# Three output projections of two model blocks: seven half-size products instead of one full product, and three VectorE steps moved

## The chip, the cores and the metric

The kernel runs on one core of a Trainium2 chip, in one launch. The metric is the device time of that core in microseconds (us). TensorE (PE) multiplies, VectorE (DVE) and ScalarE (ACT) do the element work, and SyncE (SP) issues the transfers from HBM. All data is float32.

## What is computed

A first block (a recurrent mixer and an attention mixer side by side, an output projection, then 64 experts in 8 groups) is followed by a second one (three attentions, gates, an output projection) and a last norm. There are 256 tokens (`S`) of width 1024 (`D`). The places that the change touches:

```python
# first block
y = sigmoid(gate_a) * (o_a @ w_branch_hgrn) + sigmoid(gate_b) * (o_b @ w_branch_mla)
x = x + y @ w_out                       # units wo0, wo1
h = rmsnorm(x, ffn_norm_w)
x = x + hierarchical_moe(h, ...)        # 2 of 64 experts for each token
x = rmsnorm(x, final_norm_w)
# second block
kv = rmsnorm(mem, g_mem) @ w_mem_kv     # its unit xva is computed ahead of the experts
u = gates[0] * ya + gates[1] * yb + gates[2] * yc
x = x + u @ w_out_2                     # units w20, w21
x = rmsnorm(x, g_final)
```

## The kernel before

**Units.** A weight matrix is cut into units of 512 columns: 8 blocks `k` of 128 rows, 2 MB each (`wo0` is the first half of `w_out`, `wo1` the second, `w20` and `w21` those of `w_out_2`). They pass through a ring of four slots (three in the second block); SP asks for a unit when the projection that used its slot is done.

**One list for all engines.** `plan()` writes the steps in one order; each engine runs through the list and does its part of each step, so the order of the list is the order on every engine. `("head", (unit, n))` lets TensorE do the first n products of a unit early. Projections write the psum tiles P0 and P1; `may_fill` makes TensorE wait until such a tile was read. A semaphore `full` says that a tile is written, `empty` that it was read.

**Two forms of a projection.** In the full form a unit is 16 matmuls of 512 columns (for each half `t` of the tokens, 128 each, 8 blocks k) or 32 of 256. A float32 matmul stands in the trace as two records, so 32 records of 512. The units of the list `FAST` use seven products instead (a Winograd scheme: input and weight are each seen as 2 x 2 parts, and 7 products of sums of parts give the 8 products of parts). Each product is 4 matmuls of 256 columns, or 8 of 128: 28 or 56 matmuls, 56 or 112 records. Around them VectorE does:
- `sums` (unit, 0 and 1): sums of the four weight parts, 128 x 1024 each: two in part 0 and one in part 1. In the first block the last factor, `t4`, overwrites a part of the weight, so it is a step of its own, `late`, which waits until products 2 and 1 have read that part (semaphore `made`);
- `halves`: four sums of the input's parts, 128 x 512;
- `merge` (step `proj` on VectorE): seven additions of 128 x 256 that combine the products into the result. ScalarE copies product 1 out of psum for them. The third addition frees the first of the two psum tiles.

The products run in the order 2, 1, 6, 5, 7, 3, 4; product 4 wants `t4`.

**Around the three moved steps.** During ga0 the list has 40 of its 56 matmuls, then `cnorm` (scale a 704-wide tile, transpose it, fill `cT`), the sums of the next unit ga1, ga0's `late`, then the rest of ga0. Before wb0 it has `halves` of `ob`, `gated`, `mnorm` (memT times its weight, 128 x 2048, and two small diagonals), the sums of wb1, and `late("wb0")`.

**From wo0 to the experts.** wo0 and wo1 are in the full form; VectorE adds the psum to `X` (one step of 128 x 1024 for wo0, two of 512 for wo1). `X` is transposed (xT), the router's logits (`rt`, L1444) follow, then 13 of the 16 matmuls of xva, which reads `wxva`; then the `rank` (L1714), for which VectorE must have made the router's mask (L1033), the gather (L739) and the experts' first product (L760).

**The transfers.** The experts' weights are 96 chunks of 4 MB in four buffers. SP asks for chunks 0 and 1 when wa1 and wb1 are read, chunk 2 when wb1 is full, chunk 3 when wo1 is full. `wxva` (1 MB) is asked for behind chunk 1, `fifth` (the first MB of chunk 4) behind chunk 3. The rest of chunk 4 is asked for when TensorE has read half of chunk 0 (`half_used`), and each later one when its buffer is free.

**The end.** w20 and w21 are in the full form, with heads that finish both products of the first 128 tokens first (`w2_tile`), so that their norm and output run beside the second 128. w21's second tile is done in two parts of 256 columns.

## Time and profile before

| | |
|---|---|
| median of three runs | 1581.46 us (1581.41 to 1582.23) |
| the profiled execution | 1581.34 us, its span 1579.5 us |
| TensorE busy | 1258.5 us (80%) |
| VectorE busy | 535.7 us (34%) |
| ScalarE busy | 207.0 us (13%) |
| transfers over the span | 504.48 MB read, 320 GB/s |

Times in the trace are microseconds from the start of the span. The experts take from about 346 to 1243 us; ahead of them is the first block, behind them the second. "PEclk" is the share of its full clock that TensorE was granted. A row of the chain is a piece of the longest path: start, length, what ran. TensorE's records start about 0.15 us ahead of the piece of the chain that they belong to.

### The profile page before, as it was taken

How to read it: one execution, taken by the hardware profiler on the slowest of the kernel's cores; microseconds unless marked ns; L12 is line 12 of the kernel's file. 1: busy time of each engine (PE TensorE's matmuls, PEld its weight loads, DVE VectorE, ACT ScalarE, POOL GpSimd, SP SyncE). 2: the span in 40 equal slices, each digit the busy share in tenths (PEclk: the TensorE clock that was granted, in tenths of full speed). 3: DMA queues.
4: the chain of work that ended last, by engine and by line, in shares of the span. 5: the costliest groups of instructions: out<-in, count | busy, mean ns of one | idle time of the engine just before them, and what ended most of it. 6: DMA issues, size and time to landing. Idle time of an engine off the chain costs nothing.

```text
span 1579.5 us, 20811 instructions
## 1 busy us (share of the span) xinstructions
PE 1258.5 (80%) x9150; PEld 809.5 (51%) x9150; DVE 535.7 (34%) x952; ACT 207.0 (13%) x423; POOL 2.8 (0%) x7
## 2 busy tenths in 40 slices
PE   9998999999756856756666665575666999999998
PEld 8988989853323412212212221221221488999985
DVE  5777466631000100101010010010010497798522
ACT  2002223020000000000000000000000211135311
POOL 0000000000000000000000000000000000000000
PEclk9999999999978978878878878877887999999999
DMA  9343175689999999999999999999999654434340
GB/s 371 143 161 138 60 254 192 239 350 432 437 430 434 432 434 437 430 430 440 433 428 443 430 430 441 432 433 438 430 432 428 275 213 160 161 114 167 109 160 27
DMA packets 20566, 506.58 MB, mean 321 GB/s; under 512 B 4240, under 2 KB 4368, under 8 KB 6544
## 3 DMA queue, kind: packets, MB, share of 16 engines
q1 hardware_dynamic: 20208, 505.28, 76.6%
q8 instruction: 57, 0.93, 0.2%
q10 hardware_dynamic: 288, 0.26, 0.0%
q14 instruction: 13, 0.11, 0.0%
HBM read 504.48 MB, written 1.05 MB: 320 GB/s over the span
## 4 chain that ended last, share of the span: by engine, by line
PE 54%; DMA 41%; DVE 4%; issue 1%; ACT 0%; SPq 0%; DVEq 0%; ACTq 0%
DMA ring<-in_experts 41%; PE psP L1381 13%; PE psP L760 10%; PE psP L1328 9%; PE psP L1379 9%; PE psP L808 4%; PE psA L823 2%; DVE arena L2015 1%; PE psP L1488 1%; PE psB L1707 1%; PE psB L1314 1%; DVE ring L2015 1%; PE psP L1428 0%; PE psP L1422 0%; PE psA L1661 0%
## 5 line engine op out<-in xcount | busy, mean ns | idle before, releaser
L2015 DVE TENSOR_TENSOR X<-X,psA 128x512 f32<-128x512 f32 x66 | 45.3, 688 | 696.1 <-PE psA L823 681.5
L760 PE MATMUL psP<-ring,arena 128*32 128x512 f32 x1024 | 152.2, 748 | 130.4 <-DMA ring<-in_experts 130.4
L760 PE MATMUL psP<-arena 128*32 128x512 f32 x1024 | 148.9, 733 | 128.7 <-DMA arena<-in_experts 128.5
L760 PEld LDWEIGHTS psP<-ring,arena 128*32 128x32 f32 x1024 | 38.8, 133 | 238.7 <-issue 234.9
L760 PEld LDWEIGHTS psP<-arena 128*32 128x32 f32 x1024 | 35.8, 130 | 235.5 <-DMA arena<-in_experts 120.8
L1381 PE MATMUL psP<-arena,ring 128*128 128x128 f32 x992 | 118.5, 278 | 5.2 <-DVE ring L2015 5.2
L1381 PEld LDWEIGHTS psP<-arena,ring 128*128 128x128 f32 x992 | 115.0, 194 | 6.6 <-DVE ring L2015 5.6
L808 PE MATMUL psP<-arena 128*32 128x512 f32 x512 | 66.8, 681 | 21.9 <-DMA arena<-in_experts 20.5
L808 PE MATMUL psP<-ring,arena 128*32 128x512 f32 x512 | 65.8, 666 | 22.8 <-DMA ring<-in_experts 22.0
L1381 PE MATMUL psP<-spare,ring 128*128 128x128 f32 x640 | 74.7, 275 | 0.0
L1381 PEld LDWEIGHTS psP<-spare,ring 128*128 128x128 f32 x640 | 73.0, 192 | 0.1
L739 PEld LDWEIGHTS psA<-arena 128*128 128x128 f32 x544 | 62.3, 192 | 11.9 <-issue 11.7
L2015 DVE TENSOR_TENSOR ring<-ring 128x1024 f32<-128x1024 f32 x55 | 66.5, 1221 | 1.0 <-DMA ring<-in_u_dq 0.4
L739 PE MATMUL psA<-arena 128*128 128x128 f32 x544 | 65.1, 278 | 0.0
L2015 DVE TENSOR_TENSOR arena<-arena 128x256 f32<-128x256 f32 (+6 forms) x95 | 63.6, 705 | 3.3 <-PE psB L1579 1.4
L823 PE MATMUL psA<-arena 128*128 128x512 f32 x128 | 63.4, 617 | 0.0
L1328 PE MATMUL psP<-ring,arena 128*128 128x512 f32 (+2 forms) x176 | 57.9, 487 | 0.0
L1379 PE MATMUL psP<-ring,arena 128*128 128x256 f32 x248 | 57.6, 382 | 0.0
L1328 PE MATMUL psP<-arena,ring 128*128 128x256 f32 x256 | 55.7, 379 | 0.0
L1379 PE MATMUL psP<-ring,spare 128*128 128x256 f32 x240 | 53.7, 379 | 0.2 <-issue 0.2
L972 ACT ACTIVATE arena<-psP 128x512 f32<-128x512 f32 x16 | 9.6, 597 | 335.9 <-PE psP L760 335.9
L1328 PEld LDWEIGHTS psP<-arena,ring 128*128 128x128 f32 x256 | 48.5, 190 | 6.5
(349 smaller groups left out, 1371.6 us busy)
## 6 DMA issues: line engine op xcount, KB each, us to landing
arena<-in_experts SPq DMA_DIRECT2D x7, 4096.0 KB, 21.3
ring<-in_experts SPq DMA_DIRECT2D x7, 4096.0 KB, 22.7
ring<-in_u_gl SPq DMA_DIRECT2D x6, 2048.0 KB, 8.6
ring<-in_u_hq SPq DMA_DIRECT2D x2, 2048.0 KB, 22.3
ring<-in_u_hv SPq DMA_DIRECT2D x2, 2048.0 KB, 11.7
ring<-in_u_hg SPq DMA_DIRECT2D x2, 2048.0 KB, 8.4
ring<-in_u_ga SPq DMA_DIRECT2D x2, 2048.0 KB, 8.6
ring<-in_u_gb SPq DMA_DIRECT2D x2, 2048.0 KB, 8.6
```

Of the source, the lines that this page charges most:

```text
L739: mm = pe.matmul(zA[:, k * P:(k + 1) * P], xnf[:, t, k * P:(k + 1) * P], selA[:, t].rearrange("p j c -> p (j c)"), start=(t == 0), stop=(t ...
L760: mm = pe.matmul(z[j * CAP:(j + 1) * CAP, :], x[:, 4 * half + k, j * CAP:(j + 1) * CAP], held[c % 4][:, k // 2, j, (k % 2) * 512:(k % 2 + ...
L808: mm = pe.matmul(zY[j * CAP:(j + 1) * CAP, cols * 512:(cols + 1) * 512], hidT[:, 2 * half + f, j * CAP:(j + 1) * CAP], by_columns[:, cols, ...
L823: pe.matmul(zA[:, c:c + 512], selTs[:, t * P:(t + 1) * P], rows[:, half * 512:(half + 1) * 512], start=True, stop=True).then_inc(scattered, 1)
L972: act.activation(gs, ps["P0"][:, 0:512], ACT.Silu).then_inc(gate_read, 1)
L1314: mm = pe.transpose(ps[region][:, i * P:(i + 1) * P], src_of(i), ident)
L1328: mm = pe.matmul(dsts[o], lhs_of(o, k), rhs_of(o, k), start=(k == 0), stop=(k == kc - 1))
L1379: mm = pe.matmul(z[:, at:at + 256], a[:, k, :], b[:, k], start=(k == 0), stop=(k == 3))
L1381: mm = pe.matmul(z[:, at + o * P:at + o * P + P], b[:, k, o * P:o * P + P], a[:, k, :], start=(k == 0), stop=(k == 3))
L1488: mm = pe.matmul(dsts[o], lhs, xT_raw[:, k, :], start=(k == 0), stop=(k == KC - 1))
L1707: mm = pe.matmul(dst, v, prT[:, i * nb + b, :], start=(b == 0), stop=(b == nb - 1))
L2015: return dve.tensor_tensor(o, a, b, op)
```

## The change

1. wo0, wo1 and w20 go to `FAST`. They get a product order of their own, 1, 7, 2, 6, 5, 3, 4 (`OUT_PRODUCTS`), and `seven_out` on TensorE, which waits for each factor only where it is used. VectorE's `add_out` adds the products to `X` by terms, without a separate result. For wo0 and wo1 `t4` is made inside `add_out`. `halves_a` is the one of the four input sums that needs only the first half of Y (of gl[0] for w20); `halves` makes the other three.
2. `late("ga0")` moves ahead of `cnorm`; `late("wb0")` and wb1's sums move ahead of `mnorm`.
3. `wxva` is asked for when wo1 is full, ahead of chunk 3, instead of behind chunk 1, since the new sums use its place; `fifth` waits for the squares of `X`, whose scratch now lies in its place.
4. At the end the heads of w20 and w21 are gone: w20 is done whole, then w21's first tile, its norm, and w21's second tile. The four input sums of w20 lie where those of the second block's input lay.

```diff
...
@@ -131,19 +131,21 @@
...
+OUT = ("wo0", "wo1", "w20")
...
+OUT_PRODUCTS = [(1, 0, 0), (7, 0, 256), (2, 0, 512), (6, 0, 768), (5, 1, 0), (3, 1, 256), (4, 1, 512)]
...
             p.append(("head", ("ga0", 40), ""))
+            late("ga0")
             p.append(("cnorm", 0, "AB"))
         if fill[n - 1] in before:
             sums(before[fill[n - 1]])
-        if fill[n - 1] in FIRST:
+        if fill[n - 1] in FIRST and fill[n - 1] != "ga0":
             late(fill[n - 1])
         proj(fill[n - 1])
         if fill[n - 1] == "ch":
@@ -294,16 +297,22 @@
     proj("wa1")
     p.append(("halves", "ob", ""))
     p.append(("gated", "wa1", ""))
+    late("wb0")
+    sums("wb1")
     p.append(("mnorm", 0, ""))
-    sums("wb1")
-    late("wb0")
     proj("wb0")
     late("wb1")
+    p.append(("halves_a", "y", ""))
+    sums("wo0")
     proj("wb1")
-    p.append(("head", ("wo0", 4), ""))
+    p.append(("halves", "y", ""))
+    p.append(("sums", ("wo1", 0), ""))
+    late("wo0")
+    proj("wo0")
+    p.append(("sums", ("wo1", 1), ""))
     p.append(("root_row", "mem", "A"))
-    proj("wo0")
     p.append(("xT", 0, "AB"))
+    late("wo1")
     proj("wo1")
...
-    proj("ud0", "ud1", "ux0", "ux1")
-    p.extend([("head", ("w20", 4), ""), ("head", ("w21", 4), ""), ("head", ("w20", 8), ""), ("head", ("w21", 8), "")])
+    proj("ud0", "ud1")
+    sums("w20")
+    proj("ux0")
+    p.append(("halves_a", "z", ""))
+    proj("ux1")
+    p.append(("halves", "z", ""))
+    proj("w20")
+    p.append(("head", ("w21", 8), ""))
     p.append(("final", 0, ""))
-    proj("w20", "w21")
+    proj("w21")
...
-        x_squares = area(11, NT, D)
+        x_squares = area(13, 4, 512)
...
+                        if c == 3:
+                            sp.dma_start(wxva, ins["u_xva"].rearrange("p (h k n) -> p h k n", h=2, k=KC)).then_inc(xva_in, 16)
                     else:
                         sp.wait_ge(used, c - 3)
                     sp.dma_start(dst, src).then_inc(chunk_in[c % 4], 16)
                     if c == 3:
-                        sp.wait_ge(normed, 3)
+                        sp.wait_ge(squares, 1)
                         sp.dma_start(fifth.rearrange("p e n -> p (e n)"), source(2)[:, 0:SLOT // 2]).then_inc(refill_in, 16)
-                    if c == 1:
-                        sp.dma_start(wxva, ins["u_xva"].rearrange("p (h k n) -> p h k n", h=2, k=KC)).then_inc(xva_in, 16)
...
+            def seven_out(key, arg, halves, first_in, second_in, between=None):
+                regions, w = list(USE[key]), unit_ap(arg)
+                h, s = Y if halves == "y" else gl[0], h_sums[halves]
+                t1, t2, t4 = sums_of(arg)
+                low, high = slice(0, 256), slice(256, 512)
+                factors = {1: (h[:, 0:4, 0:P], w[:, 0:4, low]), 2: (h[:, 4:KC, 0:P], w[:, 4:KC, low]),
+                           3: (s[3], w[:, 4:KC, high]), 4: (h[:, 4:KC, P:S], t4),
+                           5: (s[0], t1), 6: (s[1], t2), 7: (s[2], w[:, 0:4, high])}
+                n_halved = 4 * HALVES.index(halves)
+                for n, half, at in OUT_PRODUCTS:
+                    (a, b), z = factors[n], ps[regions[half]]
+                    if n == 1:
+                        wait_empty(pe, first_in)
+                        may_fill(pe, key, regions[0])
+                    if n == 7:
+                        pe.wait_ge(halved, n_halved + 1)
+                        pe.wait_ge(summed, SUMMED[arg])
+                    if n == 2:
+                        wait_empty(pe, second_in)
+                    if n == 6:
+                        if between:
+                            between()
+                        pe.wait_ge(halved, n_halved + 3)
+                    if n == 5:
+                        may_fill(pe, key, regions[1])
+                    if n == 3:
+                        pe.wait_ge(halved, n_halved + 4)
+                    if n == 4:
+                        pe.wait_ge(summed, SUMMED_LAST[arg])
+                    for k in range(4):
+                        mm = pe.matmul(z[:, at:at + 256], a[:, k, :], b[:, k], start=(k == 0), stop=(k == 3))
+                    if n in (7, 3):
+                        mm.then_inc(made, 1)
+                    if n in (6, 4):
+                        mm.then_inc(full[regions[half]], 1)
             rope_n = {"iq": 1, "ik": 1, "dq": 2, "dk": 3, "mq": 4, "mk": 5}
...
+                    def first_columns():
+                        wait_empty(pe, ("proj", "wo0"))
+                        for t, r in enumerate("AB"):
+                            transposes(("xT", 0), lambda i, t=t: X[:, t, i * P:(i + 1) * P], r, 4)
+                    seven_out(key, arg, "y", ("proj", "wb0"), ("proj", "wb1"), first_columns)
+                    pe.wait_ge(x_sum, 1)
+                    may_fill(pe, ("xT", 1), "A")
+                    for i in range(4, KC):
+                        tr = pe.transpose(ps["A"][:, i * P:(i + 1) * P], X[:, 0, i * P:(i + 1) * P], ident)
+                    tr.then_inc(full["A"], 1)
                 elif name == "proj" and arg == "rt":
                     pe.wait_ge(rt_scaled, 1)
...
+                    if arg == "wo0":
+                        seven_out(key, arg, "y", ("proj", "wb0"), ("proj", "wb1"))
+                        continue
+                    if arg == "w20":
+                        seven_out(key, arg, "z", ("proj", "ux0"), ("proj", "ux1"))
+                        continue
...
+            def add_out(arg, key):
+                q, (r0, r) = FAST.index(arg), list(USE[key])
+                p1, u2 = w7, w5 = kept_for(arg)
+                w, (_, t2, t4) = unit_ap(arg), sums_of(arg)
+                c = 512 * int(arg[2])
+                low, high = slice(c, c + 256), slice(c + 256, c + 512)
+                early_part = lambda at: ps[r0][:, at:at + 256]
+                late_part = lambda at: ps[r][:, at:at + 256]
+                below = X[:, 1, c:c + 512].rearrange("p (a n) -> p a n", a=2)
+                dve.wait_ge(kept, q + 1)
+                link(tt(X[:, 0, low], X[:, 0, low], p1, ALU.add))
+                wait_full(dve, key, r0)
+                link(tt(u2, early_part(768), p1, ALU.add))
+                tt(X[:, 0, low], early_part(512), X[:, 0, low], ALU.add)
+                link(tt(w7, early_part(256), u2, ALU.add))
+                dve.sem_inc(empty[r0], 1)
+                if arg in FIRST:
+                    tt(t4, w[:, 4:KC, 0:256], t2, ALU.subtract).then_inc(summed, 1)
+                link(tt(below, below, bc(w7, [P, 2, 256], 1), ALU.add))
+                dve.wait_ge(made, 2 * q + 2)
+                link(tt(w5, late_part(0), u2, ALU.add))
+                link(tt(X[:, 0, high], X[:, 0, high], w5, ALU.add))
+                dve.sem_inc(spent, 1)
+                x = tt(X[:, 0, high], late_part(256), X[:, 0, high], ALU.add)
+                if arg == "wo1":
+                    x.then_inc(x_sum, 1)
+                if arg == "w20":
+                    x.then_inc(x_done, 1)
+                tt(X[:, 1, high], late_part(0), X[:, 1, high], ALU.add)
+                wait_full(dve, key, r)
+                tt(X[:, 1, low], late_part(512), X[:, 1, low], ALU.add).then_inc(empty[r], 1)
+                dve.wait_ge(empty[r], USE[key][r])
...
+                elif name == "halves_a":
+                    wait_empty(dve, ("proj", "wb0" if arg == "y" else "ux0"))
+                    h = Y if arg == "y" else gl[0]
+                    tt(h_sums[arg][2], h[:, 0:4, 0:P], h[:, 0:4, P:S], ALU.subtract).then_inc(halved, 1)
+                elif name == "halves" and arg in ("y", "z"):
+                    s1, s2, _, s4 = h_sums[arg]
+                    n, h = 4 * HALVES.index(arg), Y if arg == "y" else gl[0]
+                    wait_empty(dve, ("proj", "wb1" if arg == "y" else "ux1"))
+                    tt(s1, h[:, 0:4, P:S], h[:, 4:KC, P:S], ALU.add).then_inc(halved, 1)
+                    dve.wait_ge(halved, n + 2)
+                    tt(s2, s1, h[:, 0:4, 0:P], ALU.subtract).then_inc(halved, 1)
+                    dve.wait_ge(halved, n + 3)
+                    tt(s4, h[:, 4:KC, 0:P], s2, ALU.subtract).then_inc(halved, 1)
...
-                    elif arg == "wo1":
-                        dve.wait_ge(wo_half, 1)
-                        tt(X[:, 0, 512:D], ps[r][:, 0:512], X[:, 0, 512:D], ALU.add).then_inc(x_sum, 1)
-                        wait_full(dve, key)
-                        tt(X[:, 1, 512:D], ps[r][:, 512:1024], X[:, 1, 512:D], ALU.add).then_inc(empty[r], 1)
                     elif arg == "w20":
-                        wait_full(dve, key)
-                        r = region_of(key)
-                        part = X[:, 1, 0:512]
-                        tt(part, ps[r][:, 512:1024], part, ALU.add).then_inc(x_done, 1)
-                        dve.wait_ge(x_done, 3)
-                        tt(xo[:, 1, 0:512], part, wrow_f[:, 0:512], ALU.mult).then_inc(x_weighed, 1)
...
-                    elif arg in ("wo0",):
-                        i = int(arg[2])
-                        wait_full(dve, key)
-                        x = tt(X[:, :, 512 * i:512 * i + 512], rows(ps[r]), X[:, :, 512 * i:512 * i + 512], ALU.add)
-                        x.then_inc(empty[r], 1)
...
-                        for i in range(2):
-                            dve.wait_ge(w2_tile, i + 1)
-                            part = X[:, 0, 512 * i:512 * i + 512]
-                            tt(part, ps[region_of(("proj", f"w2{i}"))][:, 0:512], part, ALU.add).then_inc(x_done, 1)
-                        dve.wait_ge(row_in, 32)
+                        dve.wait_ge(w2_tile, 1)
+                        part = X[:, 0, 512:D]
+                        tt(part, ps[region_of(("proj", "w21"))][:, 0:512], part, ALU.add).then_inc(x_done, 1)
```

VectorE about ga0, before: `cnorm`, three sums of ga1, ga0's `late` (the row with "made"), the first step of its merge.

```order
L2022 RECIPROCAL small<-small 128x4 [waits roots,dve_seq]
L2408 TENSOR_SCALAR arena<-arena,small 128x384 [waits dve_seq]
L2409 TENSOR_SCALAR arena<-arena,small 128x256
L2408 TENSOR_SCALAR arena<-arena,small 128x384
L2409 TENSOR_SCALAR arena<-arena,small 128x256
L2015 TENSOR_TENSOR early<-psA,consts_sb 128x5x128 [waits full_A]
L2015 TENSOR_TENSOR early<-psB,consts_sb 128x5x128 [waits full_B]
L2015 TENSOR_TENSOR spare<-ring 128x1024 [waits full_P0,full_P1,landed_3]
L2015 TENSOR_TENSOR ring<-ring 128x4x256
L2015 TENSOR_TENSOR spare<-ring,spare 128x1024 [waits summed]
L2015 TENSOR_TENSOR ring<-ring,arena 128x4x256 [waits summed,made]
L2015 TENSOR_TENSOR arena<-psP,score 128x2x128 [waits kept]
```

After, on VectorE in the same place:

```order
L2071 TENSOR_TENSOR ring<-ring,arena 128x4x256 [waits summed,made,dve_seq]
L2078 RECIPROCAL small<-small 128x4 [waits roots]
L2501 TENSOR_SCALAR arena<-arena,small 128x384 [waits dve_seq]
L2502 TENSOR_SCALAR arena<-arena,small 128x256
L2501 TENSOR_SCALAR arena<-arena,small 128x384
L2502 TENSOR_SCALAR arena<-arena,small 128x256
L2071 TENSOR_TENSOR early<-psA,consts_sb 128x5x128 [waits full_A]
L2071 TENSOR_TENSOR early<-psB,consts_sb 128x5x128 [waits full_B]
L2071 TENSOR_TENSOR spare<-ring 128x1024 [waits full_P0,full_P1,landed_3]
L2071 TENSOR_TENSOR ring<-ring 128x4x256
L2071 TENSOR_TENSOR spare<-ring,spare 128x1024 [waits summed]
L2071 TENSOR_TENSOR arena<-psP,score 128x2x128 [waits kept]
```

The `late` step went from behind the sums to ahead of the reciprocal.

VectorE about wb0, before: `gated`, `mnorm` (MEMSET to the second 128x128), wb1's sums, wb0's `late`, the merge's first step.

```order
L2015 TENSOR_TENSOR arena<-arena 128x1024
L2240 MEMSET arena 128x128 [waits memT_in]
L2015 TENSOR_TENSOR arena<-arena,consts_sb 128x2048
L2022 RECIPROCAL small<-small 128x2 [waits roots]
L2244 TENSOR_SCALAR arena<-consts_sb,small 128x128 [waits dve_seq]
L2244 TENSOR_SCALAR arena<-consts_sb,small 128x128
L2015 TENSOR_TENSOR arena<-ring 128x1024 [waits full_P0,full_P1,landed_1]
L2015 TENSOR_TENSOR ring<-ring 128x4x256
L2015 TENSOR_TENSOR arena<-ring,arena 128x1024 [waits summed]
L2015 TENSOR_TENSOR ring<-ring,arena 128x4x256 [waits summed,made]
L2015 TENSOR_TENSOR arena<-psP,score 128x2x128 [waits kept]
```

After, on VectorE in the same place:

```order
L2071 TENSOR_TENSOR arena<-arena 128x1024
L2071 TENSOR_TENSOR ring<-ring,arena 128x4x256 [waits summed,made]
L2071 TENSOR_TENSOR arena<-ring 128x1024 [waits full_P0,full_P1,landed_1]
L2071 TENSOR_TENSOR ring<-ring 128x4x256
L2071 TENSOR_TENSOR arena<-ring,arena 128x1024 [waits summed]
L2345 MEMSET arena 128x128 [waits memT_in]
L2071 TENSOR_TENSOR arena<-arena,consts_sb 128x2048
L2078 RECIPROCAL small<-small 128x2 [waits roots]
L2349 TENSOR_SCALAR arena<-consts_sb,small 128x128 [waits dve_seq]
L2349 TENSOR_SCALAR arena<-consts_sb,small 128x128
L2071 TENSOR_TENSOR arena<-psP,score 128x2x128 [waits kept]
```

`late` and the three sums stand ahead of `mnorm` now.

SP from the second wo unit to `fifth`, before:

```order
L1179 DMA ring<-in_u_wo 128x4096 [waits full_P0]
L1236 DMA arena<-in_experts 128x8192 [waits empty_P0,empty_P1] x2
L1243 DMA arena<-in_u_xva 128x2048
L1236 DMA ring<-in_experts 128x8192 [waits full_P0,full_P1]
L1236 DMA ring<-in_experts 128x8192 [waits full_P0]
L1240 DMA arena<-in_experts 128x2048 [waits normed]
```

SP in the same place, after:

```order
L1198 DMA ring<-in_u_wo 128x4096 [waits full_P0]
L1258 DMA arena<-in_experts 128x8192 [waits empty_P0,empty_P1] x2
L1258 DMA ring<-in_experts 128x8192 [waits full_P0,full_P1]
L1255 DMA arena<-in_u_xva 128x2048 [waits full_P0,full_P1]
L1258 DMA ring<-in_experts 128x8192
L1262 DMA arena<-in_experts 128x2048 [waits squares]
```

The transfer of `wxva` went from between chunks 1 and 2 to between 2 and 3, with wo1's wait.

## Rows read from the trace of the kernel before

**Rows 1.** The page: the chain that ended last, its shares by engine.

```profile
PE 54%; DMA 41%; DVE 4%; issue 1%; ACT 0%; SPq 0%; DVEq 0%; ACTq 0%
```

**Rows 2.** The chain in order of time, in the experts' stage: start, us, what.

```profile
396.28 32.04 DMA ring<-in_experts
```

**Rows 3.** Stretches: busy us (instructions) of each engine, PEclk, DMA share, GB/s.

```profile
149.40:153.00 3.60, 3.53 (x20) 3.31 (x22) 2.10 (x7) 0.00 (x0) 0.00 (x0) 0.56 0.00 0
...
430.00:470.00 40.00, 20.58 (x120) 7.55 (x116) 2.14 (x4) 2.18 (x4) 0.00 (x0) 0.75 1.02 440
```

**Rows 4.** The chain in order of time, about ga0 and ga1.

```profile
133.49 9.13 PE psP L1381 x80
...
154.22 12.70 PE psP L1381 x112
```

**Rows 5.** TensorE's instructions: start, us, line, tiles, xcount, idle before and releaser.

```profile
143.54 1.95 PE L1381 MATMUL psP<-spare,ring 128*128 128x128 f32 x16
149.47 3.48 PE L1381 MATMUL psP<-arena,ring 128*128 128x128 f32 x16 [3.98 <-DVE ring L2015]
...
290.10 5.62 PE L1381 MATMUL psP<-arena,ring 128*128 128x128 f32 x48 [1.26 <-DVE ring L2015]
...
1546.14 20.76 PE L1328 MATMUL psP<-ring,arena 128*128 128x512 f32 x48
```

**Rows 6.** VectorE's instructions, the same columns.

```profile
134.16 2.44 DVE L2015 TENSOR_TENSOR arena<-arena 128x1024 f32<-128x1024 f32 x3
138.03 0.18 DVE L2022 RECIPROCAL small<-small 128x4 f32<-128x4 f32 x1 [1.42 <-ACT small L1920]
...
148.20 1.22 DVE L2015 TENSOR_TENSOR ring<-ring,arena 128x1024 f32<-128x1024 f32 x1
...
150.12 0.42 DVE L2015 TENSOR_TENSOR score<-psP,dmask 128x256 f32<-128x256 f32 x1
...
288.82 1.22 DVE L2015 TENSOR_TENSOR ring<-ring,arena 128x1024 f32<-128x1024 f32 x1
...
290.74 0.42 DVE L2015 TENSOR_TENSOR score<-psP,dmask 128x256 f32<-128x256 f32 x1
...
1560.07 0.69 DVE L2015 TENSOR_TENSOR X<-psP,X 128x512 f32<-128x512 f32 x1 [2.74 <-PE psP L1328]
...
1562.34 1.42 DVE L2561 SCALAR_TENSOR_TENSOR arena<-X,small,arena 128x512 f32<-128x512 f32 x2
```

**Rows 7.** The chain in order of time: a unit of 56, wo0 to the router, the end.

```profile
119.98 12.28 PE psP L1379 x56
...
304.65 3.44 PE psP L1328 x8
...
333.88 0.84 PE psP L1444 x8
...
335.32 2.65 PE psP L1444 x24
...
1570.36 3.47 PE psP L1561 x16
```

**Rows 8.** TensorE's instruction that begins the rank.

```profile
341.33 0.43 PE L1714 MATMUL psB<-arena,consts_sb 128*128 128x64 f32 x2 [0.43 <-DVE arena L1033]
```

**Rows 9.** SP's issues: start, us, line, tile, count.

```profile
308.16 0.42 SPq L1243 DMA_DIRECT2D arena<-in_u_xva  x1
308.68 0.38 SPq L1236 DMA_DIRECT2D ring<-in_experts  x1
...
348.24 0.33 SPq L1228 DMA_DIRECT2D arena<-in_experts  x1
```

**Rows 10.** DMA issues from 308.1, 308.6 and 348: KB, us from issue to landing.

```profile
arena<-in_u_xva SPq DMA_DIRECT2D x1, 1024.0 KB, 15.2
...
ring<-in_experts SPq DMA_DIRECT2D x1, 4096.0 KB, 24.6
...
arena<-in_experts SPq DMA_DIRECT2D x1, 1024.0 KB, 6.0
```

82 lines of the change are left out of this document (37 added, 45 removed).

## The prediction

> **What bounds the kernel now.** I read the chain that ended last first: TensorE holds 54% of it and the transfers of the expert weights 41% [rows 1]. The chain in order of time splits the span in three. In the experts' stage it steps from one transfer to the next, for example 32.04 us of waiting for one [rows 2], with the DMA engines busy 1.02 of the time at 440 GB/s [rows 3]. A step of TensorE or VectorE inside that stage is worth nothing, but the stage is paid from its start: no chunk beyond the fifth is asked for before TensorE has read chunk 0, so whatever arrives earlier at its first product moves all of the stage. Ahead of it and behind it the chain runs on TensorE, almost without a gap. So I look for three things: the gaps of TensorE, the columns that it streams, and what the experts' first product waits for.
>
> **First moved step: late("ga0").** TensorE started ga0's next to last product at 143.54 and then stood for 3.98 us until VectorE had written the last factor, at 148.20 to 149.4 [rows 5, 6]. VectorE in that time had filled cT from the transposes and made three sums of ga1. The factor needs nothing but ga0's first two products, done near 137.1 (133.49 plus 32 of 80 records of 9.13 us [rows 4]), and VectorE is idle between its level step, which ends at 136.6, and the reciprocal at 138.03 [rows 6]. In its new place it runs from 137.1 to 138.3. It pushes cnorm's reciprocal by 0.3 us; the four scalings behind it end at 139.8 instead of 139.5, and the transposes that want them start at 142.45, so this is hidden; the cover is 2.6 us. The last product (16 records, 1.8 us at the 12.70 us for 112 of ga1 [rows 4]) then starts at 143.54 + 1.8 = 145.3 and ends at 147.1, and the level's products (1.27 us) at 148.4. What is late next is psum P1 for ga1: VectorE frees it with the third step of ga0's merge, which ended at 150.54, and the row of steps ahead of it is shorter by the factor's 1.14 us, so 149.40 [rows 6]. ga1 starts at 149.45 where it started at 154.22 [rows 4]: **-4.8 us**. That is more than the gap, because after the gap the granted clock was 0.56 and 16 records took 3.48 us, where the same number takes 1.8 us elsewhere; at the full level (2.4 GHz) these 1.7 us go as well [rows 3, 5]. The new gap at P1 is 1.1 us. A gap of 1.26 us stands ahead of 290.10, and the 48 records behind it took 5.62 us [rows 5]; at the pace of ga1 (12.70 us for 112 [rows 4]) they would take 5.44, so I take no loss of clock for it; the other end is 1.7 us. From 154 to 275 the chain is TensorE's without a wait, so the gain stays whole.
>
> The Trainium skill, page "TensorE: Matmul & The Clock Gate", section "What's actually happening", says that half rate is the default state and that only sustained work keeps the array at full rate. The trace agrees with its granted clock of 0.56 behind the gap. By it a shorter gap is a risk too and not only a cost of its own length; this is one of the rivals below.
>
> **Second and third moved steps: late("wb0") and wb1's sums ahead of mnorm.** Before wb0's last product TensorE waited 1.26 us for this factor, written from 288.82 on [rows 5, 6]. Now it is written at 282.5 to 283.7, the three sums behind it, mnorm's 2.8 us after them. The total of VectorE up to wb0's merge is the same, so P1 comes free at 291.16 as before (290.74 + 0.42 [rows 6]). wb1 started at 290.10 + 1.79 = 291.89 and starts at 291.2: **-0.7 us**, not -1.26. The sums and halves of wo0 (four steps, 4.2 us) are new on VectorE between wb1's late factor and its merge: 295.2 + 1.2 + 0.7 + 3.5 = 300.6, and TensorE needs the merge's third step only for wo0, at 303.9; it ends at 301.9. The cover is 2 us.
>
> **wo0 and wo1 by seven products.** By the full form the two took 304.65 to 333.88 = 29.23 us, of which 1.76 us are small products and transposes, and 27.5 us are 64 records of 512 columns (3.44 us for 8, 0.43 us each) [rows 7]. A unit of 56 records of 256 columns takes 12.28 us [rows 7], two of them 24.6 us: **-2.9 us**. That is a little less than the eighth of the columns that the form saves. What VectorE adds in each: eight steps of 256 or 512 columns instead of one of 1024, at 0.42 us for 256 [rows 6] and some 0.7 for 512; of these the last factor (1.2 us) counts. In wo0, products 1, 7, 2, 6 end at 311.0 (all times on the clock of the trace before); VectorE is then free from the halves and the first two sums of wo1 at 311.0, takes 1.7 us for four steps and 1.2 us for the factor: 313.9. Product 4 wants it at 314.3. In wo1 it is ready 1.2 us ahead. This is close once; bounds for it are 0 and 0.5 us a unit, and I take 0. The shorter last addition (0.42 for 0.69 us) and the transposes that now stand behind the last product (0.44 us) cancel almost. The router's logits start at 333.88 - 0.7 - 2.9 = 330.3: -3.6 us.
>
> **The weights of xva.** They were asked for at 308.16 and landed 15.2 us later at 323.4, 14 us before TensorE read them [rows 9, 10]. Now SP asks for them only when wo1 is full, at 329.8, ahead of chunk 3. The transfers of chunks 1 and 2 end by then: with 1 MB less in the queue, 24.6 us from the issue of chunk 2 become some 22.2, from 307.2 on: 329.4. One transfer of 1 MB into a queue that ran empty at 348 landed in 6.0 us [rows 10], so this one at 335.9. TensorE is there at 337.97 (335.32 + 2.65 [rows 7]) - 3.6 = 334.4 and waits 1.5 us; its 13 products take 2.9 us, to 338.8. The router's mask, on which the rank waited before, until 341.33 [rows 8], would be ready at 341.3 - 3.6 = 337.7, so the rank starts at 338.8 for 341.33: **-2.5 us instead of -3.6**. The bounds for the landing are 334.4 (no wait, -3.6) and 338.3 (two transfers share the queue: 3.6 us of latency and twice the 2.4 us of 1 MB at 430 GB/s), with which the rank starts at 341.3 as before. I take the row of 6.0 since it is the same size into the same, nearly empty queue. Behind the rank all moves with it: gather, first product, the issue at 348.24 [rows 9]. The queue then holds 1 + 4 + 1 MB from 329.8, at the rate of [rows 3] and with 3 us of latency to 347.4; the next issue comes at 345.7 and its data not before 347.7, so the stream isn't held.
>
> The Trainium skill, page "DMA: Bandwidth & Descriptors", section "Anatomy of one DMA", gives about 2.0 us plus the bytes at 436 GB/s. As an estimate from that page the transfer lands in 4.4 us, TensorE never waits and the time is 1571.4 us; the row says 6.0 us, and I go by the row.
>
> **w20 by seven products, at the end.** Before, w20 and w21 took 1546.3 to 1573.8 = 27.5 us [rows 5, 7] (a row of the instructions starts 0.15 us ahead of the chain's). Now 12.28 + 13.8 = 26.05: **-1.5 us**. The four sums (4.7 us) stand on VectorE between ud1's and ux0's steps, 1535.0 to 1539.8; ux0 is full at 1539.43, so they cost it 0.3 us, and no product wants it before 1546.3. The halves are ready at 1550.2, product 6 comes at 1551.6. The first row block's norm now waits for w21's first tile at 1565.5 instead of 1560.1 and takes 3.7 us from there (1560.07 to 1563.76 before [rows 6]), to 1569.2; w21's last product ends at 1572.4, so it is hidden by 3 us. The end behind the last product stays.
>
> **The sum**: -4.8 (ga0) - 2.5 (wb0, wo0, wo1 and xva up to the rank) - 1.5 (w20) = -8.8 us. The profiled execution took 1581.34 us, 0.12 us less than the median of the three runs, so the forecast is **1572.6 us**.
>
> **Rivals.**
> - No wait for xva, -9.9 us: **1571.4**. For it: only its landing row speaks against it. Chance 0.12.
> - xva shares the queue with chunk 3 and lands at 338.3: 2.5 us of the forecast go, **1575.0**. For it: both transfers are issued within 0.5 us. Against it: chunk 2 was issued 0.5 us behind xva before and landed at 333.3, ten us after it [rows 9, 10], so the queue went in order. Chance 0.15.
> - The clock falls in one of the two new gaps (1.1 us before ga1, 1.5 us before xva) or the factors come late: 1.7 us, or 0.5 us each: **1574.2**. For it: the half rate behind the longer gap [rows 3]. Against it: the 48 records behind the gap of 1.26 us. Chance 0.12.
> - **Slower**: xva is served behind chunk 3 and the fifth piece. It then lands 15.1 us and another 2.4 us after the issue, at 347.4; TensorE stands for 13 us, restarts at half clock (1.7 us more, as in [rows 5]) and begins the rank at 352.0, 10.7 us later than before. -4.8 + 10.7 - 1.5 = +4.4 us: **1585.7**. It decides from a landing at 345 on. Against it: the order of landing in [rows 9, 10]. Chance 0.03. The Trainium skill, page "DMA: Bandwidth & Descriptors", section "Queues, rings and completion order", says that descriptors start in ring order but completion isn't in order of issue; by it alone this case isn't excluded, and by the order seen in the trace it is unlikely.
>
> **How the numbers follow.** The forecast has 0.58; the rivals 0.12, 0.15, 0.12 and 0.03. The range 1570.2 to 1577.0 takes in the case without a wait (1571.4) with 1.2 us to spare, and above it two of the losses together (1575.0 + 1.7, less what they share); the slower case and the tails stay outside. A measurement of this kernel can tell about 0.2% (3.2 us) from no change; all cases but the slower one lie beyond that: faster 0.94, within 0.03 (two of the losses together), slower 0.03.
>
> **What the profile after would show.** Right: ga0's last 16 records at 1.8 us with a granted clock of 1.00 and ga1 starting near 149.5; no wait in wb0; 56 records of 256 columns in some 12.3 us three times; a wait of TensorE of 1 to 2 us for xva near 329.6 (334.4 less 4.8); the rank near 334; the end 1.5 us nearer to the start of w20. Wrong: a wait on VectorE at ga1 or at product 4 of wo0 over 1 us, a second stretch at half clock ahead of the experts, xva landing over 9 us after its issue, or a gap in the DMA share at the start of the experts that is longer than before.

## The result and the profile after

The changed kernel takes **1573.14 us** (median, 1572.25 to 1576.85) beside 1582.08 us (1581.41 to 1584.16) of the kernel before on the same chip: ratio 0.9948, 95% interval 0.9937 to 0.9959, 8.9 us faster. The forecast was 1572.6 us. The profiled execution took 1572.25 us (its span 1570.5 us), 9.1 us less than the profiled one of before. The changed kernel was timed twice more, on two chips: ratios 0.9940 (0.9926 to 0.9953) and 0.9950 (0.9937 to 0.9963).

First the time in which TensorE stood ahead of the experts. The first three lines of the view for the window 100 to 345 us of the changed kernel say what TensorE waited for: total, number of waits, longest.

```profile
PE psP L1400 <- DVE score L2071: 1.8, 2, 1.1
PE psP L1347 <- DMA arena<-in_u_xva: 0.6, 1, 0.6
PE psP L1440 <- DVE ring L2071: 0.2, 1, 0.2
```

The two waits on "score" are the new ones for psum P1, ahead of ga1 and of wb1; "ring" is the last factor of wo0, late by 0.22 us. The waits for factors of 3.98 and 1.26 us [rows 5] are gone; these three lines make 2.6 us together. Next TensorE's instructions in order of time, changed kernel, from ga0's fifth product to ga1 (start, duration, line, tiles, records, wait ahead of it):

```profile
142.90 1.95 PE L1400 MATMUL psP<-spare,ring 128*128 128x128 f32 x16
144.69 1.95 PE L1400 MATMUL psP<-arena,ring 128*128 128x128 f32 x16
146.56 1.21 PE L1634 MATMUL psA<-arena 128*32 128x32 f32 x64
148.90 3.81 PE L1400 MATMUL psP<-arena,ring 128*128 128x128 f32 x32 [1.13 <-DVE score L2071]
```

The last product follows at once and takes 1.95 us where it took 3.48 behind 3.98 us of standing [rows 5]. ga1 starts at 148.90 for 154.15. The windows of the same stretch (length, busy time of each engine, granted clock, share and rate of the transfers) show that the clock stays up; before it was 0.56 here [rows 3]:

```profile
146.00:150.00 4.00, 2.87 (x80) 2.66 (x79) 3.90 (x9) 0.00 (x0) 0.00 (x0) 1.00 0.57 187
150.00:155.00 5.00, 5.00 (x47) 5.00 (x46) 4.97 (x6) 2.50 (x4) 0.00 (x0) 1.00 0.23 90
```

From wo1's last products to the rank, the same view of TensorE:

```profile
309.35 1.99 PE L1440 MATMUL psP<-ring,arena 128*128 128x256 f32 x8 [0.22 <-DVE ring L2071]
...
321.30 3.62 PE L1440 MATMUL psP<-ring,arena 128*128 128x256 f32 x16
324.80 0.66 PE L1486 MATMUL psA<-consts_sb,X 128*128 128x128 f32 x4
325.29 1.01 PE L1496 MATMUL psP<-rtw,arena 128*128 128x72 f32 x8
326.13 0.60 PE L1505 MATMUL psB<-consts_sb,X 128*128 128x128 f32 x4
326.57 2.80 PE L1496 MATMUL psP<-rtw,arena 128*128 128x72 f32 x24
329.94 3.17 PE L1347 MATMUL psP<-arena 128*128 128x128 f32 x26 [0.57 <-DMA arena<-in_u_xva]
332.94 0.33 PE L1769 MATMUL psB<-arena,consts_sb 128*128 128x64 f32 x2
```

The logits start at 325.29 for 333.88 in the chain of before [rows 7] (333.72 on this clock), the rank at 332.94 for 341.33 [rows 8]: 8.4 us earlier. Then SyncE's issues (start, duration, line, tiles), changed kernel:

```profile
324.99 0.33 SPq L1255 DMA_DIRECT2D arena<-in_u_xva  x1
325.37 0.42 SPq L1258 DMA_DIRECT2D ring<-in_experts  x1
326.72 0.33 SPq L1262 DMA_DIRECT2D arena<-in_experts  x1
339.75 0.33 SPq L1247 DMA_DIRECT2D arena<-in_experts  x1
```

339.75 answers to 348.24 [rows 9]: still 8.49 us ahead. The last steps of the chain, changed kernel, from the experts' last down product on:

```profile
1236.04 1.91 PE psA L951 x4
1241.98 10.30 PE psP L1347 x24
...
1539.06 12.09 PE psP L1440 x56
1551.15 6.87 PE psP L1347 x16
1558.02 3.45 PE psA L1616 x16
1561.47 3.47 PE psP L1616 x16
```

The projection behind the experts starts at 1241.98 where it started at 1249.20 before: only 7.22 us ahead. **The experts' stage gave 1.3 us back.** The last product starts at 1561.47 for 1570.36 [rows 7]: 8.89 us, so the second block brought 1.67 us.

### The profile page after: what moved, and what is told of

The parts are those of the page before. It is cut to its first block, busy times and chain, and to the rows that moved or that the text cites. A ratio compares the mean times of both kernels' runs of the same rounds, so it can differ in the third digit from the quotient of the medians.

```text
span 1570.5 us, 21027 instructions
## 1 busy us (share of the span) xinstructions
PE 1257.4 (80%) x9222; PEld 818.6 (52%) x9222; DVE 562.7 (36%) x997; ACT 208.0 (13%) x426; POOL 2.8 (0%) x7
## 4 chain that ended last, share of the span: by engine, by line
PE 54%; DMA 40%; DVE 4%; issue 1%; ACT 0%; SPq 0%; DVEq 0%; ACTq 0%
DMA ring<-in_experts 37%; PE psP L1400 13%; PE psP L779 10%; PE psP L1398 9%; PE psP L1347 8%; PE psP L827 4%; PE psA L842 2%; DMA arena<-in_experts 2%; DVE arena L2071 2%; PE psP L1440 2%; PE psB L1762 1%; PE psB L1333 1%; DVE ring L2071 1%; PE psA L758 1%; DMA X<-in_x 1%
## 5 line engine op out<-in xcount | busy, mean ns | idle before, releaser
L779 PE MATMUL psP<-arena 128*32 128x512 f32 x1024 | 145.3, 718 | 125.6 <-DMA arena<-in_experts 125.4
L779 PEld LDWEIGHTS psP<-ring,arena 128*32 128x32 f32 x1024 | 37.8, 131 | 234.4 <-issue 229.5
L779 PEld LDWEIGHTS psP<-arena 128*32 128x32 f32 x1024 | 35.0, 129 | 230.7 <-DMA arena<-in_experts 118.6
L827 PE MATMUL psP<-arena 128*32 128x512 f32 x512 | 73.8, 741 | 22.4 <-DMA arena<-in_experts 21.0
L827 PE MATMUL psP<-ring,arena 128*32 128x512 f32 x512 | 72.8, 726 | 23.3 <-DMA ring<-in_experts 21.9
L2071 DVE TENSOR_TENSOR ring<-ring 128x1024 f32<-128x1024 f32 x61 | 73.7, 1220 | 1.1 <-DMA ring<-in_u_dq 0.5
L827 PEld LDWEIGHTS psP<-arena 128*32 128x32 f32 x512 | 18.0, 132 | 72.8 <-issue 48.5
L827 PEld LDWEIGHTS psP<-ring,arena 128*32 128x32 f32 x512 | 19.0, 130 | 69.4 <-issue 62.7
## 6 DMA issues: line engine op xcount, KB each, us to landing
ring<-in_experts SPq DMA_DIRECT2D x7, 4096.0 KB, 23.3
```

The source lines that it names most:

```text
L779: mm = pe.matmul(z[j * CAP:(j + 1) * CAP, :], x[:, 4 * half + k, j * CAP:(j + 1) * CAP], held[c % 4][:, k // 2, j, (k % 2) * 512:(k % 2 + ...
L827: mm = pe.matmul(zY[j * CAP:(j + 1) * CAP, cols * 512:(cols + 1) * 512], hidT[:, 2 * half + f, j * CAP:(j + 1) * CAP], by_columns[:, cols, ...
L2071: return dve.tensor_tensor(o, a, b, op)
```

## Experiments

**ga0's last factor alone, in the kernel before.**

```diff
             p.append(("head", ("ga0", 40), ""))
+            late("ga0")
             p.append(("cnorm", 0, "AB"))
...
-        if fill[n - 1] in FIRST:
+        if fill[n - 1] in FIRST and fill[n - 1] != "ga0":
             late(fill[n - 1])
```

> The kernel before with one step moved: VectorE writes ga0's last factor ahead of cnorm's reciprocal. My theory: the wait of 3.98 us ahead of ga0's last product goes, the 16 records behind it take 1.8 to 1.95 us instead of 3.48 with a granted clock of 1.00, and a new wait of about 1.1 us for psum P1 stands ahead of ga1; the time falls by 4.7 us, from 1582.1 to 1577.4 us. Rival, the slow 16 records have nothing to do with the wait: they stay at 3.48 us and the gain is 3.0 us, 1579.1 us. Rival, the stage of the experts takes the gain back because it runs on transfers: under 1 us gained.

Measured: 1576.83 us beside 1581.44 us of the kernel before, ratio 0.9972 (0.9961 to 0.9984), which is 4.4 us less. TensorE in that kernel:

```profile
144.93 1.95 PE L1382 MATMUL psP<-arena,ring 128*128 128x128 f32 x16
146.81 1.21 PE L1580 MATMUL psA<-arena 128*32 128x32 f32 x64
149.15 3.81 PE L1382 MATMUL psP<-arena,ring 128*128 128x128 f32 x32 [1.13 <-DVE score L2016]
```

ga0 started at 133.01 here and at 133.42 before, ga1 at 149.15 and 154.15: the move itself is worth 4.6 us. One line of the plan is half of the whole gain, and with the wait gone the 16 records take 1.95 us where they took 3.48. The rest of this trace has a surprise, told below.

**The other two moved steps undone**, in the changed kernel.

```diff
-    late("wb0")
-    sums("wb1")
     p.append(("mnorm", 0, ""))
+    sums("wb1")
+    late("wb0")
```

> The changed kernel with only the second and third moved step undone: wb0's last factor and wb1's sums stand behind mnorm again. Theory: the wait of 1.26 us ahead of wb0's last product is back, the one of 0.7 us ahead of wb1 is gone, and what follows comes 0.55 to 0.7 us later. Rival, VectorE's row is now so full that wo0's merge and halves come late as well and over 1 us is lost.

Ratio 0.9950 (0.9937 to 0.9962), 1573.14 us beside 1573.29 of the changed kernel on that chip: the times don't tell them apart. The traces do, TensorE with the steps back and then in the changed kernel beside it:

```profile
276.88 3.84 PE L1400 MATMUL psP<-arena 128*128 128x128 f32 x32 [0.20 <-DVE arena L2071]
280.56 3.74 PE L1400 MATMUL psP<-arena,ring 128*128 128x128 f32 x32
285.55 5.62 PE L1400 MATMUL psP<-arena,ring 128*128 128x128 f32 x48 [1.26 <-DVE ring L2071]
...
299.95 5.35 PE L1440 MATMUL psP<-ring,arena 128*128 128x256 f32 x24
```

```profile
276.31 3.84 PE L1400 MATMUL psP<-arena 128*128 128x128 f32 x32 [0.21 <-DVE arena L2071]
279.99 5.52 PE L1400 MATMUL psP<-arena,ring 128*128 128x128 f32 x48
286.20 3.81 PE L1400 MATMUL psP<-arena,ring 128*128 128x128 f32 x32 [0.69 <-DVE score L2071]
...
298.78 5.35 PE L1440 MATMUL psP<-ring,arena 128*128 128x256 f32 x24
```

From wb0's start to wo0's it is 23.07 us against 22.47: 0.6 us, of a wait of 1.26 us that went and one of 0.69 that came.

**w20 in the full form**, in the changed kernel: plan and code of w20 and of the end as before.

```diff
-    proj("ud0", "ud1")
-    sums("w20")
-    proj("ux0")
-    p.append(("halves_a", "z", ""))
-    proj("ux1")
-    p.append(("halves", "z", ""))
-    proj("w20")
-    p.append(("head", ("w21", 8), ""))
+    proj("ud0", "ud1", "ux0", "ux1")
+    p.extend([("head", ("w20", 4), ""), ("head", ("w21", 4), ""), ("head", ("w20", 8), ""), ("head", ("w21", 8), "")])
     p.append(("final", 0, ""))
-    proj("w21")
+    proj("w20", "w21")
...
```

> The changed kernel with w20 and w21 computed as in the kernel before, w20 in the full form of 512 columns. Theory: TensorE's last product comes 1.5 to 1.65 us later against the start of the two units and the time rises by as much, 1574.7 us beside 1573.1. Rival, VectorE's steps for w20 and the later first norm had cost the end something, so that less than 1 us comes back.

1574.31 us, ratio 0.9947 (0.9933 to 0.9960), beside 1573.14 us and 0.9940 of the changed kernel on the same chip: 1.2 us. In the traces TensorE needs 321.17 us from the projection behind the experts to the start of its last product, against 319.53: 1.64 us.

**xva's weights behind chunk 3**, in the changed kernel.

```diff
-                        if c == 3:
-
-                            sp.dma_start(wxva, ins["u_xva"]...).then_inc(xva_in, 16)
                     sp.dma_start(dst, src).then_inc(chunk_in[c % 4], 16)
                     if c == 3:
+                        sp.dma_start(wxva, ins["u_xva"]...).then_inc(xva_in, 16)
```

> The changed kernel with one transfer moved: the 1 MB of weights of xva are asked for 0.4 us behind the 4 MB of chunk 3 instead of 0.4 us ahead of it. Theory, whole transfers of SP's queue are served in the order of their issue: chunk 3 lands some 13 us after its issue, xva at about 340.6 instead of 329.9, TensorE stands for about 11 us ahead of xva's products, the router's rank and the experts' first product come 10 to 11 us later, of which the transfers give back about 1.3 us because they no longer have a queue in front of them; 1582.5 to 1584.2 us (the upper end with a fallen clock behind the wait). Rival, the two transfers share the engines evenly: xva lands at about 333.5, TensorE waits some 4 us, 1575 us. Rival, the order of the two doesn't matter: 1573.1 us.

1583.56 us beside 1581.44 us of the kernel before, ratio 1.0015 (1.0006 to 1.0024): **the whole gain and more is lost by 0.4 us in the order of two issues.** Chunk 3 landed 13.5 us after its issue, xva 15.5 us after its own, 2.4 us behind it:

```profile
arena<-in_u_xva SPq DMA_DIRECT2D x1, 1024.0 KB, 15.5
```

and TensorE, same kernel:

```profile
341.28 5.18 PE L1345 MATMUL psP<-arena 128*128 128x128 f32 x26 [11.56 <-DMA arena<-in_u_xva]
```

The two transfers landed in the order of their issue, as the theory had it; the rivals, with xva at 333.5 or with no difference, are excluded. The 26 records took 5.18 us instead of 3.17: the granted clock was 0.58 behind the wait, and that is 2.0 us more.

**Why the experts' stage grew.** The stage is measured from SyncE's issue of the first new piece (339.75 above) to the start of the projection behind it (1241.98): 902.23 us, and 900.96 before. Five kernels ask whether the transfers that stand in the queue at that issue cause it. First, the changed kernel without xva's transfer and the wait for it; it computes the second block's memory values from stale numbers, so it is no version to use:

```diff
-                        if c == 3:
-
-                            sp.dma_start(wxva, ins["u_xva"]...).then_inc(xva_in, 16)
...
-                        pe.wait_ge(xva_in, 16)
+                        pass
```

> The changed kernel without the transfer of xva's weights and without the wait for it, so the second block's memory values are computed from stale numbers: a part of the work is left out. The queue ahead of the first new piece of the experts then holds 5 MB as in the kernel before. Theory of the queue: the fifth piece lands about 2.4 us earlier, about 341, the first new piece 6 us after its issue instead of 7.8, the stage takes about 895.1 us instead of 896.3, and with 0.25 us at the rank the time is 1.4 us less than the changed kernel's. Rival, the stage's length is scatter: only the 0.25 us.

Second, the transfer asked for earlier, with chunk 3 where it was:

```diff
+                        if c == 3:
+                            sp.wait_ge(made, 2 * FAST.index("wo1") + 2)
+                            sp.dma_start(wxva, ins["u_xva"]...).then_inc(xva_in, 16)
                         before_chunk(c)
-                        if c == 3:
-
-                            sp.dma_start(wxva, ins["u_xva"]...).then_inc(xva_in, 16)
```

> The changed kernel with one transfer moved the other way: SP asks for xva's weights when product 3 of wo1 is done and not when all of wo1 is, about 1.8 us earlier, with chunk 3 where it was. Theory, the 1.3 us that the experts' stage lost come from the queue: the 1 MB of xva stands in it when the first new piece is asked for, and the piece lands 7.8 us after its issue instead of 6.0. Then with xva out of the way the piece lands about 6.3 us after its issue, the stage ends 1.3 us earlier, the wait for xva (0.57 us) is gone and the rank starts 0.25 us earlier, where the mask bounds it: 1.5 us less, 1571.6 us. Rival, the 1.3 us are scatter of one execution or come from the stage itself: only the 0.25 us, 1572.9 us, and the last product of the experts stays where it was.

Third, the same with ga1's sums moved too (its diff is further below):

> The changed kernel with both: ga1's sums in VectorE's idle stretch (the run before had the wait ahead of ga1 gone) and xva's weights asked for at product 3 of wo1 (the run before had TensorE's wait for them gone). Theory: the two gains add in the part ahead of the experts, 1.0 + 0.25 us at the rank; in the stage of the experts the earlier transfer gave nothing in the run before, so 1571.9 us by the changed kernel's 1573.1, ratio 0.9940 to the kernel before. Rival, the earlier transfer does shorten the queue and its one profile was a long one: 0.9932, another 1.3 us.

Fourth and fifth, with ga1's sums moved and the first part of chunk 3 (Q3 is 1 MB or 2 MB) asked for when wo0 is done:

```diff
+                        if c == 3:
+                            wait_full(sp, ("proj", "wo0"))
+                            sp.dma_start(dst[:, 0:Q3], src[:, 0:Q3]).then_inc(first_q, 16)
                         before_chunk(c)
...
-                    sp.dma_start(dst, src).then_inc(chunk_in[c % 4], 16)
+                    if c == 3:
+                        sp.dma_start(dst[:, Q3:], src[:, Q3:]).then_inc(chunk_in[3], 16)
+                    else:
+                        sp.dma_start(dst, src).then_inc(chunk_in[c % 4], 16)
```

> The changed kernel with ga1's sums in VectorE's idle stretch and with chunk 3 of the experts cut in two: its first 1 MB goes into the ring's slot of wo0 as soon as wo0's products are done, about 311, ahead of the stretch in which the transfer queue runs empty (busy 0.31 from 321 to 326); xva and the other 3 MB where they were. Theory of the queue: the fifth piece lands 2.4 us earlier, about 1.4 us instead of 3.8 us after the first new piece is asked for, and the stage from that issue to the projection behind the experts takes 900.6 to 901.0 us instead of 901.9; with the 1.0 us ahead of ga1 the time is 2.1 us less than the changed kernel's, 0.9927 of the kernel before. Rival, the length of the stage doesn't follow the queue: 901.9 us again, and 0.9935. Rival, the 1 MB in front delays xva's landing by up to 2.4 us, and TensorE waits 2 us more for it.

> The same with the first 2 MB of chunk 3 taken ahead instead of 1 MB. Theory of the queue in order: the 2 MB are still being served when xva is asked for, xva lands about 7 us after its issue instead of 4.9, TensorE waits about 2 us more for it and the rank comes 1.9 us later than with 1 MB; the stage takes 900.6 us. Time 1.5 to 2 us above the kernel with 1 MB. Rival, the queue is far enough ahead by then: no difference between the two.

And the changed kernel itself, twice:

> The changed kernel once more, beside the others of this group and with a second profiled execution, since the three variants of it so far differ by about as much as their runs scatter. Theory, xva's 1 MB ahead of chunk 3 lengthens the experts' stage: from the issue of the first new piece to the last down product it takes 896.3 us again, within 0.4, where the kernel before took 895.0. Rival, the 1.3 us were scatter: a length between 894.6 and 895.6 us, or beyond 896.7. The time: 0.9948 of the kernel before.

> The changed kernel beside the other three. Theory: 0.9940 to 0.9948 of the kernel before; the stage of the experts takes 901.9 to 902.2 us; the second block from the projection behind the experts to TensorE's last product takes either 319.5 us or, where the granted clock falls behind the wait of 1.75 us near 1399, 321.1 us.

The expectations for the kernel without xva and for the changed kernel's second timing count the stage to the last down product, 5.9 us less than here. Each row of this table is one profiled execution (the changed kernel has three): landing of the fifth piece against the issue of the first new piece, landing of the new piece after its issue, landing of the last expert piece after the same issue, length of the stage, all in us:

| kernel | fifth piece | new piece | last piece | stage |
|---|---|---|---|---|
| xva behind chunk 3 | -9.2 | 4.7 | 893.50 | 900.55 |
| 2 MB of chunk 3 ahead | -3.7 | 4.6 | 893.49 | 900.55 |
| 1 MB of chunk 3 ahead | -1.7 | 4.6 | 893.47 | 900.52 |
| before with ga0's factor moved | -0.1 | 4.7 | 893.47 | 901.54 |
| before | +1.2 | 6.0 | 893.91 | 900.96 |
| xva not loaded | +1.4 | 4.7 | 893.58 | 900.64 |
| both moved | +2.6 | 6.9 | 894.83 | 902.93 |
| xva earlier | +3.2 | 7.2 | 895.15 | 903.22 |
| changed kernel, three executions | +3.8, +3.8, +4.0 | 7.8, 7.4, 7.8 | 895.19, 894.80, 895.94 | 902.23, 901.85, 902.99 |
| ga1's sums moved | +3.8 | 7.2 | 894.81 | 901.86 |
| wb0's steps back | +3.8 | 7.5 | 895.26 | 902.31 |
| w20 in the full form | +4.0 | 7.5 | 894.87 | 901.92 |

The rows fall in two groups. Where the queue is empty, or nearly, when the first new piece is asked for, the mean of the six stages is 900.8 us; where the fifth piece lands 2.6 us or more after that issue, the mean of the eight is 902.4 us, and no execution lies in the other group's span. The last piece separates them more clearly: 893.5 to 893.9 us against 894.8 to 895.9 us. In the changed kernel xva itself lands 9.8 us ahead of that issue; it is the fifth piece, pushed back by xva's 1 MB, that the new piece stands behind. Here is the new piece as landing after its issue (changed kernel, then the one without xva):

```profile
arena<-in_experts SPq DMA_DIRECT2D x1, 1024.0 KB, 7.8
```

```profile
arena<-in_experts SPq DMA_DIRECT2D x1, 1024.0 KB, 4.7
```

In three rows a part of the stage isn't the queue's. From the last landing to the projection behind the experts it is 7.05 us in 11 of the executions and 8.1 us in the kernel before with ga0's factor moved, with both moved and with xva earlier. There the granted clock fell behind a wait for the piece next to the last (0.68 over the 32 records behind it, 1.00 in the other executions). TensorE with xva earlier, then in the changed kernel:

```profile
1215.21 5.34 PE L779 MATMUL psP<-arena 128*32 128x512 f32 x32 [3.32 <-DMA arena<-in_experts]
```

```profile
1215.42 3.64 PE L779 MATMUL psP<-arena 128*32 128x512 f32 x32 [2.99 <-DMA arena<-in_experts]
```

Those 1.7 us bring TensorE to the last piece 1.1 us after it landed, where it stands ready in the other executions, so these three stages are 1.0 us longer than their transfers make them.

So the theory of the queue holds: the kernel without xva has ratio 0.9931 (0.9918 to 0.9945), 1570.91 us beside 1573.14, which is 2.2 us less where I expected 1.4, and three kernels that load xva but meet an empty queue have the short stage too. Its size isn't exact: the changed kernel's own three executions differ by 1.1 us (the third, at 902.99, lies outside the 901.9 to 902.2 that I expected). And my expectation for the kernel with xva earlier failed. Asking for xva 1.9 us earlier took TensorE's wait away, yet the fifth piece landed only 0.7 us earlier (342.76 for 343.50) and the last piece 895.15 us after the first request, as in the changed kernel; 1572.36 us, ratio 0.9940 (0.9927 to 0.9954). With both moved it was 1572.60 us, 0.9934 (0.9920 to 0.9947). And in the kernel with 1 MB of chunk 3 ahead the stage took 900.5 us, near the expected 900.6 to 901.0, but xva came late:

```profile
310.20 0.33 SPq L1259 DMA_DIRECT2D ring<-in_experts  x1
323.78 0.33 SPq L1262 DMA_DIRECT2D arena<-in_u_xva  x1
...
342.64 0.33 SPq L1252 DMA_DIRECT2D arena<-in_experts  x1
```

```profile
331.21 4.79 PE L1357 MATMUL psP<-arena 128*128 128x128 f32 x26 [3.05 <-DMA arena<-in_u_xva]
```

The 1 MB asked for at 310.20 landed at 326.4, since chunks 1 and 2 were before it; xva landed 7.4 us after its issue instead of 4.8. The issue at 342.64 is 3.9 us later than with ga1's sums alone (338.72): 2.6 us more of waiting and 1.6 us of fallen clock behind it, less 0.3 us by which ga0 started earlier in this execution. Ratio 0.9949 (0.9934 to 0.9963). With 2 MB it was the same, 3.15 us of waiting, 0.9951 (0.9938 to 0.9964), not 2 us later: my rival that the two wouldn't differ was the right one, but not for its reason, since xva landed 7.4 and 7.5 us after its issue in both. Why the second MB cost nothing more stays open. The low share of the transfer engines ahead of xva's issue (0.31 from 321 to 326 in the changed kernel, where chunk 2 landed at 325.6) didn't mean that 1 MB more would land in time.

**A better version: ga1's sums ahead of the steps that wait for cnorm's transposes.** VectorE's code of cnorm is cut in two plan entries, so that its four scalings go first, then ga1's sums, then the two copies to cT.

```diff
                     i.then_inc(normed, 1)
+                elif name == "cfill":
+                    key = ("cnorm", 0)
                     for t, r in enumerate("AB"):
...
             sums(before[fill[n - 1]])
+        if fill[n - 1] == "ga0":
+            p.append(("cfill", 0, ""))
```

> The changed kernel with ga1's three sums on VectorE ahead of the two steps that wait for cnorm's transposes, in the 3.2 us in which VectorE stood there. Theory: psum P1 is freed before TensorE wants it, the wait of 1.13 us ahead of ga1 goes and all behind it moves with it: 1.1 us less, 1572.0 us. Rival, ga0's merge is not held by the steps ahead of it but by its own products: the wait stays over 0.7 us and the time within 0.4 us of 1573.1.

1571.44 us, ratio 0.9940 (0.9926 to 0.9954). TensorE in that kernel, no wait ahead of ga1:

```profile
144.94 1.95 PE L1402 MATMUL psP<-arena,ring 128*128 128x128 f32 x16
146.82 1.21 PE L1636 MATMUL psA<-arena 128*32 128x32 f32 x64
147.95 3.84 PE L1402 MATMUL psP<-arena,ring 128*128 128x128 f32 x32
```

ga0 starts 0.25 us later than in the changed kernel's first trace and ga1 0.95 us earlier: 1.2 us. The first new piece is asked for at 338.72 for 339.75. It beats the kernel before clearly; that it beats the changed kernel, by about 1.2 us, rests on the traces, since the intervals of the two ratios overlap.

## Why the prediction was right, step by step

- **What bounds the kernel.** Held: every move outside the experts' stage came through at full size at the stage's start, and the stage itself is paid by transfers.
- **ga0, -4.8 us forecast.** 4.6 us: the wait, the half clock behind it and the new wait of 1.1 us (measured 1.13) all as worked out.
- **wb0 and wb1, -0.7 us forecast.** 0.6 us: the wait of 1.26 us became one of 0.69.
- **wo0 and wo1, -2.9 us forecast.** 2.5 us (29.23 to 26.69 us from wo0's first record to the logits). The factor of wo0, called "close once" with bounds 0 and 0.5 us, was late by 0.22 us: its row of VectorE steps was a little longer than summed.
- **xva's landing: mis-sized.** I took 6.0 us from the row of a transfer of the same size and a wait of 1.5 us; it landed 4.9 us after its issue and TensorE waited 0.57 us. That cost next to nothing, since the mask was ready only at 332.69, 0.25 us ahead of the rank: the first new piece is asked for 14.46 us behind the logits' start, and 14.36 us where xva comes earlier and the mask is what the rank waits for. The row of 6.0 was a long one: in five of the kernels above the same piece took 4.6 to 4.7 us, in one of them with the fifth piece still 1.4 us from landing, where it was 1.2 us in the kernel before; what made it 6.0 there is open. The rank gained 8.4 us, 7.7 without the early start below, where the sum had 7.3. The estimate of 4.4 us from the Trainium skill, page "DMA: Bandwidth & Descriptors", section "Anatomy of one DMA", was 0.5 us from the 4.9 us, the row I chose 1.1 us; but that section is on transfers that GpSimd issues, and these are SyncE's, so the closeness proves little.
- **"So the stream isn't held": this step failed.** I let the queue run dry at 347.4 and the next data start at 347.7, on the clock of the trace before. But because TensorE waited less, the issue came 14.8 us behind xva's and not 15.9, and the six MB took 18.5 us to land and not 17.6: chunk 2, which I had landing 0.4 us ahead of xva's issue, took 23.3 us and not 22.2 and landed 0.6 us behind it. So the fifth piece landed 3.8 us behind the issue where I had 1.7, and the new piece stood behind it. That cost 1.3 us in the pair of traces and 1.6 us in the means of the table. Ahead of the stage things went nearly as in the rival without a wait for xva (1571.4 us); the price in the stage stood in none of the cases.
- **w20, -1.5 us forecast.** 1.64 to 1.67 us (its 56 records took 12.09 us and not 12.28); the sums, the halves and the later first norm were hidden as said.
- **The rest is scatter that the sum can't hold:** ga0 starts anywhere from 132.69 to 133.77 in the profiled executions, without a cause in the change, and the changed kernel's first trace had an early one (132.77 for 133.42).

The sum of the traces: -0.65 (start) - 4.6 - 0.64 - 2.54 to the logits, -0.06 from there to the first new piece, +1.27 in the stage, -1.67 behind it: -8.9 us. That the forecast's -8.8 agrees so closely is in part luck: two errors of about 1.2 us, xva's landing and the queue, cancel, and in this pair of traces the early start covers the 0.6 us by which ga0, wb0, wo0 and wo1 gave less than forecast. The **slower** rival was a real one: with the order of the two issues turned, TensorE stands for 11.6 us (13 by the sum), begins the rank at 346.3 (352.0 less ga0's 4.8, 347.2, by the sum), and the time is 1583.6 us (1585.7). That the transfers land in order was read from two rows of the trace before [rows 9, 10], and it held in every kernel here.

## What to carry to other kernels

Where two engines hand work back and forth, look for a step that stands behind others without needing them, and count what the standing costs behind it too: here 1.5 of 4.6 us were fallen clock. In front of a stage that is bound by transfers a megabyte isn't free just because TensorE doesn't wait for it, nor because it has itself landed in time: if it pushes others back so that they still stand in the queue at the stage's first request, the stage is longer, here by 1.3 to 1.6 us for 1 MB. And before a longer stage is put down to transfers, compare the landing of its last piece: 1.0 us of three stages here was TensorE's clock. And a landing that is sized by one row can be off by over 1 us: where it decides, look for several rows of its size.
